# Divisions moved ahead of the later scores, residual rows loaded one at a time, the last short stretch written out with the first mixed parts inside it, and smaller first loads, in a fused encoder-layer kernel

## What is computed

```python
z = einsum('bld,dc->blc', h, w_in)              # one projection, 2048 -> q, k, v, gates of both groups of heads
fo = fox_prompt(fq, fk, fv, lf) * silu(fg)      # 16 heads, causal, scores + c_q - c_k (forget terms)
so = swa_prompt(sq, sk, sv, sinks, rel) * silu(sg)  # 16 heads, windows of 64-frame chunks, bias, sink
out = einsum('blc,cd->bld', concatenate([fo, so], -1), w_out)
y = layer_norm(ALPHA * h + out, ln_g, ln_b)     # and the keys, values and forget terms are returned
```

## Time and profile before

| | |
|---|---|
| median of 3 runs | 1112.52 us (1111.88 to 1113.66) |
| the profiled execution's own time | 1112.64 us |
| its span | 1111.1 us |
| PE busy | 1065.3 us, 96% of the span |
| DVE busy | 610.9 us, 55% |
| ACT busy | 435.5 us, 39% |
| mean granted clock of TensorE | 0.993 |
| moved by DMA | 106.61 MB, mean 96 GB/s |

### The profile page before, as it was taken

The page is one execution under the profiler, slowest core; times in us unless marked ns, Lnnn a source line. Parts: engine busy times, 40 slices in busy tenths (PEclk is TensorE's granted clock), DMA queues, the critical chain, the costliest instruction groups (busy, mean ns, idle before and its releaser), DMA issues.

```text
span 1111.1 us, 20622 instructions
## 1 busy us (share of the span) xinstructions
PE 1065.3 (96%) x7617; PEld 985.5 (89%) x7617; DVE 610.9 (55%) x1490; ACT 435.5 (39%) x1075; POOL 50.4 (5%) x99
## 2 busy tenths in 40 slices
PE   7999999999999999999998999998999898999996
PEld 6999999999999999999997888998888776788885
DVE  6655364645545454554546557455576473424486
ACT  5344444434444444444445435344444453012300
POOL 1010000000000000000000000000000000000000
PEclk9999999999999999999999999999999999899998
DMA  8132312231232222223512111222112127222423
GB/s 335 42 131 88 109 65 101 97 104 58 89 108 86 69 97 104 89 76 114 177 51 87 59 70 45 87 86 82 54 45 76 45 76 246 76 76 76 160 87 113
DMA packets 20375, 106.61 MB, mean 96 GB/s; under 512 B 3168, under 2 KB 3584, under 8 KB 11056
## 3 DMA queue, kind: packets, MB, share of 16 engines
q1 hardware_dynamic: 14528, 83.12, 21.0%
q0 software_dynamic: 5808, 22.95, 6.1%
HBM read 95.18 MB, written 14.17 MB: 98 GB/s over the span
## 4 chain that ended last, share of the span: by engine, by line
PE 84%; DVE 9%; issue 3%; DMA 2%; ACT 1%; DVEq 0%; SPq 0%; ACTq 0%; POOLq 0%
PE ps L1132 53%; PE ps L1275 17%; PE ps L1223 5%; PE ps L1245 5%; DVE small L881 2%; DVE tb L867 2%; PE ps L1207 2%; PE ps L1206 2%; DVE tb L898 1%; DMA rows<-in_x_s 1%; DVE wl L789 1%; PE ps L1160 1%; DVE small L894 1%; DVE small L892 1%; PE ps L1259 1%
## 5 line engine op out<-in xcount | busy, mean ns | idle before, releaser
L1132 PE MATMUL ps<-xh,wh 128*128 128x288 f32 (+1 forms) x1664 | 506.7, 304 | 0.1
L1132 PE MATMUL ps<-xl,wh 128*128 128x288 f32 (+1 forms) x1664 | 493.4, 297 | 0.0
L1132 PE MATMUL ps<-xh,wl 128*128 128x288 f32 (+1 forms) x1664 | 492.9, 296 | 0.0
L1132 PEld LDWEIGHTS ps<-xh,wh 128*128 128x128 f32 x1664 | 313.6, 188 | 9.2 <-issue 7.2
L1132 PEld LDWEIGHTS ps<-xl,wh 128*128 128x128 f32 x1664 | 313.9, 189 | 0.0
L1132 PEld LDWEIGHTS ps<-xh,wl 128*128 128x128 f32 x1664 | 313.4, 188 | 0.0
L789 DVE TENSOR_TENSOR wl<-w_raw,wh 128x1024 fp32r<-128x1024 f32 x132 | 160.1, 1221 | 71.2 <-ACT wh L613 68.4
L1275 PE MATMUL ps<-wh,mix_parts 128*128 128x512 f32 x576 | 188.8, 397 | 7.7 <-DVE rows L1062 4.9
L613 ACT ACTIVATE wh<-w_raw 128x1024 fp32r<-128x1024 f32 x132 | 137.9, 1053 | 84.7 <-PE ps L1275 77.9
L660 ACT ACTIVATE tb<-tb,small 128x256 f32<-128x256 f32 (+5 forms) x160 | 82.4, 515 | 221.6 <-DVE small L877 132.1
L1275 PEld LDWEIGHTS ps<-wh,mix_parts 128*128 128x128 f32 x576 | 110.1, 191 | 31.3 <-DVE rows L1062 5.3
(11 more groups left out here) (112 smaller groups left out, 822.4 us busy)
## 6 DMA issues: line engine op xcount, KB each, us to landing
w_raw<-in_w_all SPq DMA_DIRECT2D x66, 1024.0 KB, 4.8
cbc<-c_rows POOLq DMA_DIRECT2D x16, 360.0 KB, 4.1
x_raw<-in_xT SPq DMA_DIRECT2D x8, 592.0 KB, 9.5
rows<-in_x_p POOLq DMA_DIRECT2D x4, 1024.0 KB, 9.7
out_y_p<-rows SPq DMA_DIRECT2D x16, 256.0 KB, 2.5
rel_copies<-rel_rows POOLq DMA_DIRECT2D x1, 3072.0 KB, 15.6
out_fvT<-vT POOLq DMA_DIRECT2D x8, 296.0 KB, 2.4
out_fkT<-kT POOLq DMA_DIRECT2D x8, 296.0 KB, 2.4
```

Of the source, the lines that this page charges most:

```text
L1132: ins = nc.tensor.matmul(ps[:, st.bank(k, h), 0:width], a[k % 2][:, w], b[:, ko, first:first + width], start=(ko == 0 and i == 0), stop=(k ...
```

## The change

It has five parts, and the computation is the same.

1. In every stretch VectorE's `reciprocals` of a step are issued ahead of its `scores`, not behind them.
2. The queries' semaphore `q_high` counts each head, so that VectorE can begin with the first head when ScalarE is at the second.
3. The last short stretch is taken out of the loop and written out. At its step 15 ScalarE and VectorE split chunk 0 of the mixed output, behind a new semaphore `x_passed` that TensorE raises when it has read chunk 3 in the last half tile. The first groups of the final stretch come in the order 0, 2, 3, 4, 1 of token tiles.
4. POOL loads each block of residual rows as soon as the chunks that it covers are split (4, 8, 11, 15 and 16 chunks), with a semaphore for each, and `add_residual` waits for its own.
5. The first two chunks of x are loaded one by one and the next as before in twos, and the first halves of the two first weight tiles are loaded as two quarters each.

```diff
-X_PARTS = 8
+X_CUTS = [0, 1, 2, 4, 6, 8, 10, 12, 14, 16]
+X_PARTS = len(X_CUTS) - 1
...
-                with engine.Fori(first + 1, first + 4) as g:
+                with engine.Fori(first + 1, first + (4 if m == 0 else 3)) as g:
                     run(Stretch("gq", 2 * g + (n0 + 2 - 2 * first), own=Swa, pair=g, kind=Swa, g=g - 1,
                                 kvs=FOX_PAIRS + m + 1, turn_before=g - 2, keep=True))
+            run(Stretch("gq", PROJ_TILES - 2, own=Swa, pair=PAIRS - 1, kind=Swa, g=PAIRS - 2, kvs=KV_SETS,
+                        turn_before=PAIRS - 3, keep=True, last=True))
...
-        opening = [("x", 0), ("w", 0), ("w", 1), ("x", 1), ("x", 2), ("x", 3), ("w", 2), ("w", 3)]
-        opening += [("x", i) for i in range(4, X_PARTS)]
+        opening = [("x", 0), ("w", 0), ("w", 1), ("x", 1), ("x", 2), ("w", 2), ("w", 3), ("x", 3), ("x", 4), ("w", 4),
+                   ("w", 5)] + [("x", i) for i in range(5, X_PARTS)]
...
-            over = -(-4 * D_MODEL // NQ)
             for m in range(MT):
-                if m in (0, 4):
-                    pool.wait_ge(mix_high, over if m == 0 else KO)
-                    pool.wait_ge(mix_low, over if m == 0 else KO)
+                over = min(-(-(m + 1) * D_MODEL // NQ), KO)
+                pool.wait_ge(mix_high, over)
+                pool.wait_ge(mix_low, over)
                 src = x_p[m * P:(m + 1) * P, :] if m < 4 else x_s
-                pool.dma_start(rows[row_range(m), m, :], src).then_inc(rows_loaded, 16)
+                pool.dma_start(rows[row_range(m), m, :], src).then_inc(rows_loaded[m], 16)
...
             def run(st):
-                if st.final:
-                    mixed_high(0)
...
+                    if st.last and s == 15:
+                        act.wait_ge(x_passed, 1)
+                        mixed_high(0)
...
-                    dve.wait_ge(q_high, 2 * st.pair + h + 1)
                     for head in range(2):
+                        dve.wait_ge(q_high, 4 * st.pair + 2 * h + head + 1)
...
+                    if st.last and s == 15:
+                        mixed_low(0)
...
+                    for u in st.at(st.score_at, s - 2):
+                        reciprocals(st, u)
                     for u in st.at(st.score_at, s):
                         scores(st, u)
-                    for u in st.at(st.score_at, s - 2):
-                        reciprocals(st, u)
...
-            dve.wait_ge(rows_loaded, 16 * MT)
             with dve.Fori(1, NT - 1) as nt:
                 for m in range(MT):
+                    dve.wait_ge(rows_loaded[m], 16)
                     add_residual(nt - 1, m, m, m)
...
+                    elif st.last and k == 1 and h == 1 and ko == 3:
+                        ins.then_inc(x_passed, 1)
...
                     if ko == 0:
+                        m = (0, 2, 3, 4, 1)[m]
```

More of the change, by code:

```diff
@@ L198, in __init__ @@
     def __init__(self, tiles, n0, own=None, pair=None, kv=None, kind=None, g=None, kvs=None,
-                 turn_before=None, keep=False, first=False, final=False):
+                 turn_before=None, keep=False, first=False, last=False, final=False):
         self.tiles, self.n0, self.own, self.pair, self.kv = tiles, n0, own, pair, kv
         self.kind, self.g, self.kvs = kind, g, kvs
-        self.turn_before, self.keep, self.first, self.final = turn_before, keep, first, final
+        self.turn_before, self.keep, self.first = turn_before, keep, first
+        self.last, self.final = last, final
         self.steps = OUT_STEPS if final else STEPS * len(tiles)
@@ L349, in build @@
         wff_high, wff_low = sem("wff_high"), sem("wff_low")
-        w_half_loaded = [sem(f"w_half_loaded{i}") for i in range(4)]
+        w_part_loaded = [sem(f"w_part_loaded{i}") for i in range(6)]
+        w_quarter_high, w_quarter_low = sem("w_quarter_high"), sem("w_quarter_low")
         w_loaded = [sem("w_loaded0"), sem("w_loaded1")]
@@ L376, in build @@
         mix_high, mix_low = sem("mix_high"), sem("mix_low")
-        rows_loaded, norm_loaded = sem("rows_loaded"), sem("norm_loaded")
+        x_passed = sem("x_passed")
+        rows_loaded, norm_loaded = [sem(f"rows_loaded{m}") for m in range(MT)], sem("norm_loaded")
         out_tile_done = sem("out_tile_done")
@@ L696, in opening_splits @@
                         slot, a = w_part(i)
[L697 to L698 removed]
+                        act.wait_ge(w_part_loaded[i], 16)
+                        nc.scalar.activation(wh[slot][:, a], w_raw[slot][:, a], ACT.Copy
+                                             ).then_inc(w_quarter_high if i < 2 else w_high, 1)
                 gates()
@@ L935, in opening_splits @@
                         slot, a = w_part(i)
-                        dve.wait_ge(w_high, i + 1)
+                        if i < 2:
+                            dve.wait_ge(w_quarter_high, i + 1)
+                        else:
+                            dve.wait_ge(w_high, i - 1)
                         nc.vector.tensor_tensor(wl[slot][:, a], w_raw[slot][:, a], wh[slot][:, a].bitcast(F32),
-                                                ALU.subtract).then_inc(w_low, 1)
+                                                ALU.subtract).then_inc(w_quarter_low if i < 2 else w_low, 1)
                 dve.wait_ge(small_loaded, 4 * 16)
@@ L1006, in run @@
             def run(st):
-                if st.final:
-                    mixed_low(0)
                 if st.kind:
@@ L1164, in opening_products @@
                     for k in range(2):
-                        if i % 4 == 0:
-                            pe.wait_ge(w_low, 2 * (i // 4) + k + 1)
+                        if chunks.start == 0:
+                            pe.wait_ge(w_quarter_low, k + 1)
+                        elif chunks.start % 4 == 0 and chunks.start <= KO // 2:
+                            pe.wait_ge(w_low, 2 * (chunks.start // 8) + k + 1)
                         if k == 0 or i < X_PARTS - 2:
```

12 lines of the change are left out of this document (6 added, 6 removed).

## The result

The changed kernel takes 1078.95 us at the median of 4 runs (1078.43 to 1079.56), against 1112.8 for before in the same comparison: a ratio of 0.9696, 95% interval 0.9679 to 0.9713. The profiled execution took 1078.65 us, with a span of 1077.1 and mean granted clock 0.997.

What follows compares the result with a forecast made beforehand. TensorE's waits, plus the slow clock behind the two longest inside the program, were taken as the bound; 12.4 + 1.3 + 4.4 + 7.8 + 1.3 - 1.2 = 26.0, so 1112.6 - 26.0 = 1086.6 us, range 1082.5 to 1092.

Steps and rivals of the forecast that it cites:

- The start of the final stretch: Splitting chunk 0 early removes 2.7 of TensorE's 2.77 us wait there, and 1.7 us of slow clock behind it.
- the residual rows: Ahead of the second output tile, earlier loads remove TensorE's 4.9 us wait and 2.9 us of slow clock: 7.8 us.
- the opening: At the kernel's start, smaller first loads let TensorE begin near 6.4 us and end 1.3 us ahead.
- the opening gains nothing: Rival, chance 0.12: a half load holds the queue as long as a whole one at the start; 1088.5 us.
- the fifth block is late: Rival, chance 0.07: the fifth load of residual rows stays slow by itself, so 2 us stay; 1088.5 us.
- slower than before: Rival, chance 0.02: divisions wait for unfinished exponentials in all 160 units, delaying scores; 1118.6 us at 0.2 us each.
- so the time falls by what goes from these waits and by nothing else: Whole kernel: TensorE is otherwise fed, so only its listed waits' idle time can be gained; slow clock priced separately.
- Divisions ahead of scores: -12.4 us: Six short stretches: dividing in VectorE's idle time removes 12.4 of 13.7 us of TensorE's waits for divided rows.
- Query heads one by one: -1.3 us: Ahead of a pair's first scores: starting VectorE behind the first head removes four TensorE waits of 0.33 us, 1.3 us.
- with TensorE's steps at their unstalled 2.25 us: Short stretches: a count at this step length put the third division up to 0.3 us late, others in time.
- VectorE is the bound: Rival, chance 0.12: order does not matter in the short stretches, half of thirty waits stay, 6 us less gained; 1092.5 us.
- New in the final stretch: +1.2 us: Final stretch: divisions first delay the row maximum and so the turned copies, three of nine times 0.4 us.

Runs made afterwards that it cites:

- the experiment: Kernel before with only the last short stretch written out, chunk 0 split in it and its order of first groups: 1108.35 us (0.9964).
- the residual rows alone: Kernel before with only each block of residual rows loaded when its chunks are split: 1104.14 us (0.9925).

## Why the prediction was wrong

**Right: the places, and the mechanism at three of them.** The start of the final stretch (forecast 2.7 and 1.7 of clock; alone 4.0 measured, 2.9 in the ledger for the gap), the residual rows (7.8; 7.9 in the ledger) and the opening (1.3; 1.2 in the ledger) came out as summed, and in the changed kernel the clock stayed up as forecast. The estimate of 15.4 us for the third part took its fit from "Anatomy of one DMA" of the Trainium skill's page "DMA: Bandwidth & Descriptors", which gives it for DMAs that GpSimd issues; these are SP's, and ScalarE had the part at 10.84. Of the rivals, "the opening gains nothing" and "the fifth block is late" are out by the traces above. So is "slower than before". The one wait that the last part was to leave, a few tenths, is 0.3 in the experiment and absent from TensorE's list in the changed kernel, where only its weight load waits 0.3 us.

**Wrong: the price and the number of the short waits.** The step that failed is the first one, "so the time falls by what goes from these waits and by nothing else". From it follow "Divisions ahead of scores: -12.4 us" and "Query heads one by one: -1.3 us", 13.7 together; the ledger has 20.4 in their place, and alone they measured 17.3 and 2.5. A row's idle time begins where the matmul ahead is shown to end, though the next could have started before that, and it says nothing of the slower start behind it: that is 4.6 us for the 24 listed waits for divided rows and 0.4 for the four ahead of first scores. And TensorE's list leaves the shortest waits out: twelve of them gave another 3.3 us. The second place where this went wrong is "with TensorE's steps at their unstalled 2.25 us", which is a step of 2.59 less its idle 0.34. Steps of the same stretch in the changed kernel:

```profile
792.50 0.38 PE L1237 MATMUL ps<-ident,tb 128*128 128x128 f32 x2
...
794.55 0.40 PE L1237 MATMUL ps<-ident,tb 128*128 128x128 f32 x2
...
797.31 0.44 PE L1237 MATMUL ps<-ident,tb 128*128 128x128 f32 x2 [0.53 <-DVE tb L905]
...
799.47 0.41 PE L1237 MATMUL ps<-ident,tb 128*128 128x128 f32 x2
```

A step without idle time takes 2.05 us (792.50 to 794.55), or 2.16 (797.31 to 799.47), not 2.25. The stretch as a whole went from 38.02 us to 34.57. This could have been read in the trace of before. Ahead of the turn at 816.27 with its 0.34 us stand these two:

```profile
815.51 0.29 PE L1132 MATMUL ps<-xl,wh 128*128 128x288 f32 x1
815.64 0.29 PE L1132 MATMUL ps<-xh,wl 128*128 128x288 f32 x1
```

They start 0.13 apart, so the turn could have started at 815.77 by that pace, and it came 0.50 us behind that. (Its counterpart at 799.47 in the changed kernel, without a wait, starts 0.18 behind the matmul ahead, so 0.45 of the 0.50 are the wait's.) Either is more than the 0.34 of the list. The weight loads' list with its 43 waits was there to be read too.

**Too small: what VectorE couldn't hide.** The forecast left 1.3 us in the list, of a third division up to 0.3 late. There are 2.9, one wait of about 0.5 in each of the six short stretches. VectorE there (start, duration):

```profile
795.38 1.22 DVE L796 TENSOR_TENSOR wl<-w_raw,wh 128x1024 fp32r<-128x1024 f32 x1
...
796.90 0.35 DVE L905 TENSOR_SCALAR tb<-tb,small 128x256 f32<-128x256 f32 x1
797.17 0.42 DVE L874 TENSOR_TENSOR tb<-ps,bias 128x256 f32<-128x256 f32 x1
```

A weight split of 1.22 us stands ahead of the division, and VectorE has no idle time here. So the rival "VectorE is the bound" is right for one unit of the stretch, and not for the others. This took 1.6 us the other way, which hid part of the error above: 12.1 us of listed idle time went where 13.7 were forecast, and 8.3 came beside it.

**Not there: "New in the final stretch: +1.2 us".** The changed kernel has the same single wait of 0.5 us for a copy as before, and the old order there changes nothing. Why the copies' slack was larger than counted was not followed further.

So the sum with the sizes of the ledger is 20.4 for the first two terms, 2.9 + 1.6 for the start of the final stretch with nothing for the new wait, 7.9 and 1.2, in place of 12.4 + 1.3, 4.4 - 1.2, 7.8 and 1.3.

## What to carry to other kernels

Price a wait of TensorE by the starts of its matmuls, not by the idle time in the list: take the start of the one ahead, add the pace of its neighbours, and see how late the next one starts and how much slower the one behind it follows. Many short waits are worth far more than their sum in the list, and some stand in no row of it; count them in the weight loads' list, or look for a matmul that is longer than others of its shape. Before a surplus is divided by a number of waits, compare the starts one by one: here 6.6 us over 24 waits looked like 0.28 each, and were 0.19 each and six waits that TensorE's list doesn't have. Two long waits with the clock behind them, on the other hand, were priced rightly by the list and a window.

## What the runs showed of the hardware

- A wait of TensorE costs more than its idle row: 0.19 us more for each of 24 waits of turns (128 columns) taken away, 0.29 more for each of 32 put in ahead of 512-column matmuls. Of it 0.16 lie under the matmul ahead, and the rest mostly in a slower start behind, 0.03 to 0.06 behind a turn and 0.11 at 512 columns. Why the start behind is slower is open.
- Waits that leave no idle row on TensorE cost up to 0.28 us: 12 of 0.28 for divided rows, 32 of 0.28 put in, 7 of 0.19 for keys. All of them stand in the weight loads' list.
- After gaps of 2.77 and 4.89 us TensorE's granted clock fell to 1.2 GHz (0.50) in the kernel before. The longer gap did so in each of the five traces that have it; behind the shorter it fell in four traces and stayed at 1.00 in that of the residual rows alone. After a gap of 1.67 us, which the changed kernel still has, it stood at 1.00 from the first matmul on:

```profile
586.67:589.00 2.33, 2.33 (x18) 2.33 (x19) 2.11 (x5) 0.00 (x0) 0.04 (x1) 1.00 0.33 130
```
